# Even layer of an encoder trunk: five attention stages against 72 unrolled tile steps on one Trainium2 core

## What is computed

```python
aq, ak, av, bq, bk, bv = split_cols(h @ w_in, (A_W, A_W, A_W, B_W, B_W, B_W))   # six times 512 columns
...
# A, differential attention: 4 heads, each two score maps of 64 features, one value of 128
s = einsum('...qhcd,...khcd->...hcqk', q, k) * DH_A ** -0.5 + bias
p = softmax(where(valid, s, NEG))
a = p[..., 0, :, :] - lam * p[..., 1, :, :]
oa = rms_norm(einsum('...hqk,...khe->...qhe', a, v), subln_g) * out_scale
...
# B, chunk-band attention: 8 heads of 64 features, at most 8 chunks of 64 keys to the left
ob = softmax(q @ k * d ** -0.5 + bias, band) @ v
...
mix = concatenate([oa, ob], -1)
x = layer_norm(ALPHA * x + mix @ w_out)
```

## Time and profile before

| | |
|---|---|
| three runs | 3517.25, 3521.65, 3524.36 us, median 3521.65 |
| profiled execution, own time | 3521.4 us |
| its span (first to last instruction) | 3519.6 us |
| mean granted TensorE clock | 0.914 of full speed |
| busy in the span | PE 87%, PEld 80%, DVE 43%, ACT 27%, POOL 24% |
| even layer's mixer: first matmul / end of its last product | 90.61 us / about 893 us |
| DMA over the span | 128.80 MB, 37 GB/s |

### The profile page before, as it was taken

How to read it: one execution, slowest core, us unless ns; L and a number is a source line. 1 busy time by engine, 2 the same in 40 slices (tenths; PEclk the granted TensorE clock), 3 DMA queues, 4 the chain that set the end, 5 groups by cost and what they waited for, 6 DMA issues and landing times.

```text
span 3519.6 us, 49427 instructions
## 1 busy us (share of the span) xinstructions
PE 3046.1 (87%) x18006; PEld 2812.2 (80%) x18153; DVE 1512.5 (43%) x3607; ACT 935.9 (27%) x2258; POOL 832.2 (24%) x425
## 2 busy tenths in 40 slices
PE   1788889888699999999876777689996999999996
PEld 1777778888599999999754565578876999999994
DVE  1445543444522322332438888843543322232233
ACT  2444444444411011101232222244443101101113
POOL 0122122111133243334101111012112343334330
PEclk8899999999899999999967666699998999999998
DMA  5111011111011111111000001010000111111101
GB/s 120 40 44 44 26 46 40 39 33 31 18 48 42 42 48 47 48 36 54 15 11 17 16 16 29 1 33 22 21 19 24 42 48 48 42 42 48 48 30 49
DMA packets 197964, 128.80 MB, mean 37 GB/s; under 512 B 24435, under 2 KB 180403, under 8 KB 197875
## 3 DMA queue, kind: packets, MB, share of 16 engines
q1 hardware_dynamic: 185104, 121.87, 11.5%
q10 hardware_dynamic: 12770, 5.79, 1.1%
HBM read 110.28 MB, written 17.34 MB: 36 GB/s over the span
## 4 chain that ended last, share of the span: by engine, by line
PE 69%; DVE 15%; ACT 6%; issue 6%; ACTq 1%; DMA 1%; another core or an unknown queue 1%; POOL 1%; SPq 0%; DVEq 0%; POOLq 0%; PEldq 0%
PE ps L734 19%; PE ps L735 19%; PE ps L736 19%; PE ps L846 5%; DVE sel_mask L1396 4%; PE ps L758 3%; DVE Y L1566 2%; ACT xf L1270 2%; PE ps L958 1%; DVE yc L1623 1%; PE ps L1032 1%; PE ps L809 1%; PE ps L811 1%; DVE sd L1621 1%
## 5 line engine op out<-in xcount | busy, mean ns | idle before, releaser
L734 PE MATMUL ps<-Xh,w_hi 128*128 128x352 f32 (+1 forms) x3024 | 990.9, 328 | 126.2 <-PEq L919 77.5
L735 PE MATMUL ps<-Xl,w_hi 128*128 128x352 f32 (+1 forms) x3024 | 978.9, 324 | 0.0
L736 PE MATMUL ps<-Xh,w_lo 128*128 128x352 f32 (+1 forms) x3024 | 978.5, 324 | 0.0
L631 POOL TENSOR_TENSOR w_hi<-w_raw,zero 128x1024 fp32r<-128x1024 f32 x186 | 351.5, 1890 | 2558.6 <-PE ps L736 1261.6
L734 PEld LDWEIGHTS ps<-Xh,w_hi 128*128 128x128 f32 (+1 forms) x3024 | 574.6, 190 | 131.4 <-issue 62.8
L735 PEld LDWEIGHTS ps<-Xl,w_hi 128*128 128x128 f32 (+1 forms) x3024 | 575.4, 190 | 0.5
L736 PEld LDWEIGHTS ps<-Xh,w_lo 128*128 128x128 f32 (+1 forms) x3024 | 573.5, 190 | 0.5
L633 POOL TENSOR_TENSOR w_lo<-w_raw,w_hi 128x1024 fp32r<-128x1024 f32 x186 | 449.3, 2416 | 14.6
L1659 DVE TENSOR_TENSOR hid_f<-ps,gate_s 128x352 f32<-128x352 f32 x132 | 69.3, 525 | 811.8 <-PE ps L736 811.8
L1666 DVE TENSOR_TENSOR Y<-ps,Y 128x352 f32<-128x352 f32 x528 | 274.5, 523 | 212.7 <-PE ps L736 212.7
L734 PE MATMUL ps<-Hh,w_hi 128*128 128x352 f32 x1056 | 343.7, 325 | 9.9 <-DVE Hl L1661 9.9
(11 more groups left out here) (224 smaller groups left out, 3974.3 us busy)
## 6 DMA issues: line engine op xcount, KB each, us to landing
w_raw<-in_w_ffn_in_dram SPq DMA_DIRECT2D x176, 256.0 KB, 3.1
w_raw<-in_w_ffn_out_dram SPq DMA_DIRECT2D x88, 256.0 KB, 2.8
w_raw<-in_w_in_even_dram SPq DMA_DIRECT2D x48, 256.0 KB, 3.9
w_raw<-in_w_in_odd_dram SPq DMA_DIRECT2D x26, 256.0 KB, 3.4
x_in<-in_x_prompt_dram SPq DMA_DIRECT2D x8, 512.0 KB, 7.5
w_raw<-in_w_out_even_dram SPq DMA_DIRECT2D x16, 256.0 KB, 2.8
w_raw<-in_w_out_odd_dram SPq DMA_DIRECT2D x16, 256.0 KB, 3.7
out_dram<-Y SPq DMA_DIRECT2D x8, 512.0 KB, 2.9
```

The source lines that it names most:

```text
L631: pool.tensor_tensor(view(WH[w][:, :]), raw, zeros, ALU.add).then_inc(S["w_split"], 1)
L734: pe.matmul(out, wh, hi, start=first, stop=False)
L735: pe.matmul(out, wh, lo, start=False, stop=False)
L736: return pe.matmul(out, wl, hi, start=False, stop=last)
```

## The change

The five stages of the even layer become one phase `EV` that is written out as 72 steps, nine query tiles for each of the eight groups, behind a head of nine projection jobs for the first group. In step n PE issues: the scores of tile n; one projection job, the one nine further on, so that a group's attention carries the next group's whole projection; one small group of other transposes (keys of the next group, its cached keys, or the output of the group before); the probability transposes of tile n-1; and the values of tile n-1. Before, values followed two steps behind.

Other parts of it:

- Value jobs are no longer feature-major. A token tile of `Xh` or `Xl` is stationary and 128 weight columns move, so that values come out token-major and their nine transposes and copies go. A group's value jobs become 96, 96 and 24 matmuls of 128 moving columns, where they were three times 24 of 352. Key and query jobs keep 24 matmuls each, over chunks of 384, 384 and 288 tokens.
- The down projections go. The outputs of groups 0 to 5 are stored to DRAM (`o_park`) and loaded into `Xh` and `Xl` at the end; those of groups 6 and 7 are written there directly. One output projection of 24 jobs of 24 matmuls follows the last step, and `Y` is added to 24 times (192 before).
- `Y` is not resident in the phase. SETUP writes ALPHA times x into a ring of four (`ystage`), SP stores it to DRAM (`y_park`, 18 transfers), and it is loaded back before the output projection.
- Keys, values and bias rows have two slots each, so that the next group's can be written during attention. Two PSUM banks take transposes in turn, one takes the running job.
- On ACT, a step is: exponentials of tile n, the copies of the job, the copies of the side group, the probability copies of tile n-1, the output rows of tile n-1.

```diff
+EV_KINDS = "AAAABBBB"
+EV_STEPS = TILES * len(EV_KINDS)
+EV_CHUNKS = [(0, 3 * P), (3 * P, 3 * P), (6 * P, T - 6 * P)]
...
-STAGES = {"A0": (1, None, None, "A", 0, True), "AL": (3, "A", 0, "A", 1, True),
-          "AE": (1, "A", 3, "B", 0, True), "BL": (3, "B", 0, "B", 1, True), "BE": (1, "B", 3, None, None, False),
...
-            for name in MIXERS["AB"]:
-                stage(name, sp, stage_loads)
...
+                for g in range(X_GROUPS):
+                    sp.wait_ge(S["setup_xh"], g + 1)
+                    t, half = g // 2, g % 2
+                    nq = P if t < NT else DEC
+                    sp.dma_start(y_park[:, 4 * half:4 * half + 4, t * P:t * P + nq], ystage[:, g % 4, :, 0:nq]).then_inc(S[f"e_yst{g % 4}"], 16)
...
+                for g in range(EV_LAST - 1):
+                    for half, buf in enumerate((Xh, Xl)):
+                        sp.dma_start(buf[:, g, :].bitcast(F32), o_park[g, half]).then_inc(S["e_old"], 16)
...
+                        for t in TM_ALL[i - 3]:
+                            rows = DEC if t == NT else P
+                            out = bank[0:rows, t % 4 * P:t % 4 * P + P]
+                            for k in range(KB):
+                                wh, wl = WH[w][:, k * P:(k + 1) * P], WL[w][:, k * P:(k + 1) * P]
+                                xh, xl = Xh[:, k, t * P:t * P + rows], Xl[:, k, t * P:t * P + rows]
...
+                                pe.matmul(out, xh, wh, start=(k == 0), stop=False)
+                                pe.matmul(out, xl, wh, start=False, stop=False)
+                                mm = pe.matmul(out, xh, wl, start=False, stop=(k == KB - 1))
...
+                for n in range(EV_STEPS + 1):
+                    groups = len(prob_blocks(n - 1)) if n else 0
+                    if n < EV_STEPS:
+                        score(n, 0)
+                        score(n, 1)
+                    if n + TILES < EV_STEPS:
+                        job(n + TILES)
+                    if n < EV_STEPS:
+                        side(n)
+                    for k in range(groups):
+                        prob_transposes(n - 1, k)
+                        if k:
+                            values(n - 1, k - 1)
+                    if groups:
+                        values(n - 1, groups - 1)
...
+                for o in range(3 * KB):
+                    u = 3 * len(EV_KINDS) + o // 3
...
+                    for k in range(KB):
+                        mm = three(ps[:, EV_HEAD_BANKS[o % 5], 0:CH], e_unit_slot(u), k, Xh[:, k, c * CH:(c + 1) * CH],
+                                   Xl[:, k, c * CH:(c + 1) * CH], k == 0, k == KB - 1)
...
+                for n in range(EV_STEPS + 1):
+                    groups = len(prob_blocks(n - 1)) if n else 0
+                    if n < EV_STEPS:
+                        exps(n)
+                    if n + TILES < EV_STEPS:
+                        job(n + TILES)
+                    if n < EV_STEPS:
+                        side(n)
+                    for k in range(groups):
+                        prob_rows(n - 1, k)
+                    if n:
+                        output_rows(n - 1)
```

More of the change, by code:

```diff
@@ new lines, with key_tiles, prob_blocks @@
+EV_KINDS = "AAAABBBB"
+EV_LAST = len(EV_KINDS) - 1
+TILES = NT + 1
+EV_STEPS = TILES * len(EV_KINDS)
+EV_CHUNKS = [(0, 3 * P), (3 * P, 3 * P), (6 * P, T - 6 * P)]
+EV_TILES = [[0, 1, 2], [3, 4, 5], [6, 7, NT]]
+EV_BLOCKS = P_MAPS["B"] * -(-(5 * P) // P)
+EV_PART = dict(units=3 * len(EV_KINDS) + KB, jobs=TILES * len(EV_KINDS) + 3 * KB)
+EV_HEAD_BANKS = [7, 0, 1, 2, 3]
+def key_tiles(kind, c):
+    return [t for t in EV_TILES[c] if kind == "A" or t >= 4]
+def prob_blocks(n):
+    kind = EV_KINDS[n // TILES]
+    nk = tile_spec(kind, n % TILES)[3]
+    blocks = [(m, j) for m in range(P_MAPS[kind]) for j in range(len(key_blocks(nk)))]
+    return [blocks[a:a + 4] for a in range(0, len(blocks), 4)]
@@ new lines, in side_group, with transpose_order @@
+def side_group(n):
+    g, t = n // TILES, n % TILES
+    if t in (1, 2, 3) and g < EV_LAST and key_tiles(EV_KINDS[g + 1], t - 1):
+        return ("k", g + 1, t - 1)
+    if t == 4 and g < EV_LAST:
+        return ("cache", g + 1, 0)
+    if t in (5, 6, 7) and g > 0:
+        return ("o", g - 1, t - 5)
+    return None
+def transpose_order():
+    order = [("k", 0, c) for c in range(3)] + [("cache", 0, 0)]
+    for n in range(EV_STEPS + 1):
+        groups = range(len(prob_blocks(n - 1))) if n else []
+        if n < EV_STEPS and side_group(n):
+            order.append(side_group(n))
+        order += [("p", n - 1, k) for k in groups]
+    return order + [("o", EV_LAST, k) for k in range(3)]
@@ L467, in x_group, with e_tbank, e_evicted, e_unit_slot @@
             return src, (slice(None), slice(4 * half, 4 * half + 4), slice(t * P, t * P + nq))
+        def e_tbank(key):
+            return ps[:, 4 + EV_T[key] % 2, :].rearrange("p (j c) -> p j c", j=4)
+        def e_evicted(key):
+            return S[f"e_tev{EV_T[key] % 2}"], EV_T[key] // 2 + 1
+        def e_unit_slot(u):
+            return (BASE["EV"]["units"] + u) % 2
+        def e_jobs(j):
+            return BASE["EV"]["jobs"] + j
+        def e_prob(n, m):
+            width = SEQ if EV_KINDS[n // TILES] == "A" else 5 * P
+            return eProb[:, n % 2, m * width:(m + 1) * width]
+        def e_bias(g, m):
+            width = WINDOW[EV_KINDS[g]] * P
+            return eBias[g % 2][:, m * width:(m + 1) * width]
+        def e_out(n):
+            return ps[:, 6, n % 4 * P:n % 4 * P + P]
+        def e_job_bank(j):
+            return ps[:, EV_HEAD_BANKS[j % 5] if j < TILES else 7, :]
+        def e_key_columns(c):
+            first, n = EV_CHUNKS[c]
+            prompt = min(n, SEQ - first)
+            spans = [(0, prompt, first)]
+            return spans + [(prompt, DEC, SEQ + PAST)] if prompt < n else spans
+        def e_output(g, k):
+            cols = slice(k * 4 * P, min((k + 1) * 4 * P, T))
+            if g < EV_LAST - 1:
+                n = cols.stop - cols.start
+                return eOTh[:, 0:n], eOTl[:, 0:n]
+            return Xh[:, g, cols], Xl[:, g, cols]
         def output_group(buf, n):
@@ L700, in mixers, with even_layer, split, settled @@
                     stage(name, pool, stage_splits)
-            mixers("AB")
+            def even_layer():
+                before("EV", "pool", pool)
+                for n in range(2):
+                    pool.memset(eV[n][:, NT + PAST // P, :], 0.0).then_inc(S["e_zero"], 1)
+                    pool.memset(eO[:, n, NT, :], 0.0).then_inc(S["e_zero"], 1)
+                units = 3 * len(EV_KINDS)
+                steps = [0]
+                def split(u):
+                    n, slot = BASE["EV"]["units"] + u, e_unit_slot(u)
+                    pool.wait_ge(w_loaded[slot], n // 2 * 32)
+                    if u >= 2:
+                        old = u - 2
+                        pool.wait_ge(S["d_done"], e_jobs(3 * (old + 1)))
+                    raw = w_raw[:, slot, :]
+                    pool.tensor_tensor(WH[slot][:, :], raw, zero[:, 0:1].to_broadcast([P, D_MODEL]), ALU.add).then_inc(S["w_split"], 1)
+                    pool.wait_ge(S["w_split"], n * 2 + 1)
+                    pool.tensor_tensor(WL[slot][:, :], raw, WH[slot][:, :].bitcast(F32), ALU.subtract).then_inc(S["w_split"], 1)
+                def settled(ins):
+                    steps[0] += 1
+                    ins.then_inc(S["e_pool"], 1)
+                def mask(part, p0):
+                    pool.wait_ge(S["e_pool"], steps[0])
+                    z = zero[p0:p0 + HD, 0:1].to_broadcast([HD, HD])
+                    n = neg[p0:p0 + HD, 0:1].to_broadcast([HD, HD])
+                    settled(pool.tensor_tensor(part, z, n, ALU.add))
+                def fill_bias(q):
+                    kind = EV_KINDS[q]
+                    width = WINDOW[kind] * P
+                    pool.wait_ge(S[f"e_bld{q % 2}"], 16 * sum(B_MAPS[k] for k in EV_KINDS[q % 2:q + 1:2]))
+                    for m in range(B_MAPS[kind]):
+                        rows = e_bias(q, m)
+                        if steps[0]:
+                            pool.wait_ge(S["e_pool"], steps[0])
+                        far = rows[:, width - NEAR:width - NEAR + 1].to_broadcast([P, width - NEAR])
+                        settled(pool.tensor_tensor(rows[:, 0:width - NEAR], zero[:, 0:1].to_broadcast([P, width - NEAR]), far, ALU.add))
+                        mask(rows[0:HD, width - HD:width], 0)
+                        if kind == "B":
+                            mask(rows[HD:P, 0:HD], HD)
+                    pool.wait_ge(S["e_pool"], steps[0])
+                    pool.sem_inc(S["e_bok"], 1)
+                split(0)
+                split(1)
+                fill_bias(0)
+                split(2)
+                split(3)
+                for g in range(EV_LAST):
+                    split(3 * g + 4)
+                    fill_bias(g + 1)
+                    split(3 * g + 5)
```

(3 more changed lines are left out.)

503 lines of the change are left out of this document (491 added, 12 removed), and 1 row of the table STAGES.

## The result

The changed kernel takes 3740.85 us (median of four runs, 3739.77 to 3741.21) against 3520.98 us in the same comparison: ratio 1.0631, 95% interval 1.0616 to 1.0645. The forecast was 3664 us. Its sign was right, the measured time lies just inside the range (3555 to 3745), and the loss is 220 us where 143 were forecast.

A forecast was written before the change was run, and what follows sets the result against it. PE's work and waits were taken to bound the kernel. Work 699 plus waits 175 gave 874 us, 940 at clock 0.93, 137 above 803; with 6 us for SETUP, 3521.4 became 3664 us, range 3555 to 3745.

The forecast's parts named there:

- Value jobs: PE's value projection: 0.115 us per matmul of 128 moving columns, 11 us more per group, 88 in eight.
- Down projection: 92 us of products leave the groups, 92 us come back in the output projection: no gain on PE.
- Waits: PE's waiting in the even layer: 175 us after the change, 40 more than before, with ACT's queue deciding a step.
- the allowance for handovers: Within the waits: some three late handovers a step; with the side copies, 20 us taken for a B group.
- Clock: Even layer: half-clock share stays 14%, so 874 us become 940 at 0.93; ends 901 (0.97) and 1040 us (0.84).
- The rival *Clock: Value jobs stream little, so half-clock share doubles to 28%: +213, 3741 us; chance 0.10 shared with chains (*Nothing is hidden*).
- Transfers: Loads and stores: nothing for weights and returning outputs; 6 us for the Y store in SETUP, ends 0 and 28.
- Groups: Group times in the even layer: A about 97 us, B 107, the last about 67.
- Nothing is hidden: Steps run as chains with 31 us of waits in every group: +228, about 3755 us; chance 0.10 shared with clock.
- Faster: Value matmuls follow after 0.06 us and waits are absorbed: 34 us less in the phase, about 3493; chance 0.08.
- its point that decides: Even layer: the kernel gets faster only if work plus waits stay below 747 us.

The follow-up runs named there:

- value jobs as products: The change, but value jobs are again products of a standing weight block against 384, 384 and 288 tokens, with nine transposes a group; 3624.6 us, ratio 1.0303.
- side group first: The change, but DVE makes the side group's low parts ahead of the job's, and ACT copies the side group ahead of the job; 3744.6 us, ratio 1.0627.
- early, ACT late: The change with two probability transpose groups ahead of the job on PE, but ACT's probability copies still behind exponentials and job copies; 3692.9 us, ratio 1.0508.
- early: The change, but the first two probability transpose groups go ahead of the projection job, and ACT copies them before the exponentials; 3525.2 us, ratio 1.0023.
- early, products: The change with both early probability transposes and copies, and value jobs as products of a standing weight block; 3432.65 us, ratio 0.9761.

## Why the prediction was right or wrong

| kernel | phase, us | clock | at half clock | work | waiting |
|---|---|---|---|---|---|
| before | 803 | 0.93 | 112 | 612 | 135 |
| the change | 1004 | 0.86 | 281 | 699 | 164 |
| value jobs as products | 896 | 0.87 | 233 | 615 | 165 |
| side group first | 1009 | 0.84 | 323 | 699 | 149 |
| early, ACT late | 960 | 0.89 | 211 | 699 | 155 |
| early | 790 | 0.98 | 32 | 699 | 75 |
| early, products | 703 | 0.98 | 28 | 615 | 74 |

- *Value jobs: right.* 0.115 us from start to start was taken, 0.11 is in the trace; the form is worth 92.5 us where 84 were reckoned. One reading was wrong, though the sum did not use it: no stationary block of the scores in the earlier trace rows was loaded while PE waited. The product ahead of them started at 238.88 us and the first score at 239.04, with no wait shown, and the blocks of the first two scores were loaded from 238.88 and 239.04 us on. The Trainium skill's 81 ns ("TensorE: Matmul & The Clock Gate", "Back-to-back issue gap") does not hold for this stream: the trace has 0.11 us, as the scores had the earlier trace rows.
- *Down projection: right.* The output projection takes 95 us (92), dense.
- *Waits: the sum right, a part missed.* 175 us were forecast, 164 measured. ACT's order was the mechanism named. Missed was DVE's side of it, the shared transpose bank, 78 us by the view of waits; the allowance for handovers happened to cover it, which is luck.
- *Clock: this step failed.* "I leave the share at half clock at 14%, as it is." It was 28%, 141 us of loss where 66 were forecast, and that is nearly the whole error of the sum (75 of 77 us). The rival *Clock* gave 3741 us with just this doubling, but for a reason that the runs refute as the main one: without the form of the value jobs the share is 26%, with the form and without the waits 4%. The trace of before had the sign of it: the stretch with a quarter of its time idle had 0.84 and the denser ones 0.95 and 0.97. I read these as ends of a range and took the middle; the change spread the waits over every step, and so the phase came out near the end that I had called the worst.
- *Transfers: mis-sized.* 6 us of SETUP were forecast, 19 measured. I reckoned with shared bandwidth; but the stores stood behind the bias rows already queued, and the first four reuses of the ring of four waited 8 to 11 us each for one. Behind the last wait ACT had copies to make until 104.4 us, which before lay under the wait for the bias rows. About 5 us of the 19 are the first weight split, which moved behind the phase's start; I had counted the splits as hidden.
- *Groups:* 97, 107 and 67 us were forecast; A takes 103 once running, B 113 to 139, the last 86, at a clock of 0.62.

The rival *Nothing is hidden* did not happen, and *Faster* never came near, though its point that decides, work plus waits below 747 us, is the right measure: early transposes with products have 689.

## What to carry to other kernels

When a change alters where TensorE waits, cost the waits together with the clock: here 80 to 90 us of waiting brought 90 to 125 us of half-clock loss with them, and taking them away gave both back. In an interleaved step, look at every engine's queue for what stands ahead of a copy that TensorE waits for, and put that copy, and the transposes that feed it, ahead of the long job, which then hides them. To free the shared bank alone gave nothing here. Before giving a resident buffer away to DRAM, look at which transfers are already queued when its stores are issued.

## What was not expected of the hardware

A clock that has fallen can stay down through long value jobs (96 matmuls of 128 moving columns, another stationary block of 128 x 128 each time). Windows of the change: the first products of the phase; the two long value jobs of group 5 and what stands between and behind them; the short value job behind them; and what follows it:

```profile
110.00:114.00 4.00, 4.00 (x13) 4.00 (x14) 0.00 (x0) 0.00 (x0) 3.92 (x2) 0.52 0.48 134
114.00:118.00 4.00, 4.00 (x25) 4.00 (x24) 0.24 (x1) 1.35 (x3) 1.80 (x3) 1.00 0.45 132
705.00:735.00 30.00, 29.68 (x136) 28.69 (x135) 3.00 (x15) 5.15 (x14) 0.00 (x0) 0.50 0.10 28
735.00:763.00 28.00, 26.14 (x120) 25.45 (x120) 1.90 (x6) 4.11 (x9) 0.00 (x0) 0.50 0.00 0
763.70:765.80 2.10, 2.10 (x21) 2.10 (x22) 1.00 (x4) 0.87 (x3) 0.00 (x0) 0.50 0.00 0
765.80:769.20 3.40, 2.42 (x25) 2.19 (x24) 0.86 (x2) 2.42 (x7) 2.73 (x2) 1.00 0.38 113
```

The products of 384 columns that open the phase at half clock are at full clock 4 us later. In group 5 PE is shown as busy for 56 of 58 us, and the clock stays at 0.50, while the same jobs entered at full clock keep it (25 us at 1.00 in the run with early transposes). It rose 2.1 us into the short value job, whose stationary block has 32 columns and whose matmuls follow each other after 0.11 us at half clock, not 0.21. So the busy share of the view does not tell whether the clock will rise.

The form of the job alone does not tell it either. In the run with ACT's copies late the clock was down from 690 us, through scores and transposes, and rose 1.8 us into a long value job that had begun at 691.5:

```profile
690.00:693.30 3.30, 3.30 (x17) 3.10 (x15) 1.64 (x8) 1.52 (x4) 0.74 (x1) 0.50 0.02 5
693.30:696.70 3.40, 3.40 (x32) 3.40 (x31) 0.07 (x1) 0.00 (x0) 0.00 (x0) 1.00 0.00 0
```

In group 5 of the change the clock fell at 704.4 us, just as the first long value job began (704.55); in groups 4 and 6 these jobs began at full clock. Why it fell there and not in the others was not tried.
